# Banded attention by pairs of heads with block-diagonal keys

## What is computed

```python
def sliding_window_attention(q, k, v, sinks, rel_bias_table):   # S=512, BLOCK=WINDOW=128
    qb = q.reshape(B_, nb, BLOCK, Hkv, G, d)
    kb, vb = banded(k), banded(v)                # each block with the block before it: 256 keys
    logits = einsum('bnqkgd,bnskd->bnkgqs', qb, kb) * d ** -0.5
    logits = where(valid, logits + bias, -inf)   # bias by distance and head; valid: rel in [0, 128)
    m = maximum(max(logits, axis=-1), sink)
    p = exp(logits - m)
    p = p / (sum(p, axis=-1) + exp(sink - m))
    return einsum('bnkgqs,bnskd->bnqkgd', p, vb)
```

## Time and profile before

| what | value |
|---|---|
| median of 3 runs | 2322.81 us (2321.84 to 2324.82) |
| the profiled execution | 2321.14 us |
| its span | 2319.2 us |
| mean granted TensorE clock | 0.928 |
| PE busy | 2104.6 us (91%), 9984 instructions |
| DVE, ACT, POOL busy | 1028.7, 757.4, 157.8 us |

### The profile page before, as it was taken

The page is one execution under the profiler, slowest core; times in us unless marked ns, Lnnn a source line. Parts: engine busy times, 40 slices in busy tenths (PEclk is TensorE's granted clock), DMA queues, the critical chain, the costliest instruction groups (busy, mean ns, idle before and its releaser), DMA issues.

```text
span 2319.2 us, 25487 instructions
## 1 busy us (share of the span) xinstructions
PE 2104.6 (91%) x9984; PEld 1717.6 (74%) x9984; DVE 1028.7 (44%) x1463; ACT 757.4 (33%) x1130; POOL 157.8 (7%) x179
## 2 busy tenths in 40 slices
PE   6999999999999899999999998997439888999898
PEld 5865777888788687778887877775339666888786
DVE  4321434343336645344333345455543337665434
ACT  3125323222224455332222242434213224333322
POOL 2000000000002201000000022000002012000000
PEclk8989679999999999899999998999569999999998
DMA  5210012322232101132232223021020022223231
GB/s 167 91 37 0 1 55 84 97 90 90 91 105 71 58 19 37 37 93 91 90 106 86 98 73 101 19 63 47 18 55 1 1 73 73 90 90 105 76 101 44
DMA packets 137004, 158.11 MB, mean 68 GB/s; under 512 B 15832, under 2 KB 125408, under 8 KB 136928
## 3 DMA queue, kind: packets, MB, share of 16 engines
q1 hardware_dynamic: 135632, 155.01, 21.0%
q0 software_dynamic: 1296, 2.05, 0.3%
HBM read 153.36 MB, written 3.68 MB: 68 GB/s over the span
## 4 chain that ended last, share of the span: by engine, by line
PE 86%; DVE 8%; ACT 2%; POOL 1%; issue 1%; DMA 1%; SPq 0%; DVEq 0%; ACTq 0%; POOLq 0%
PE bank L2196 30%; PE bank L1940 16%; PE bank L2217 15%; PE bank L2016 4%; PE bank L2044 3%; PE bank L1964 3%; PE bank L2032 2%; PE bank L2081 2%; POOL arena L752 1%; PE bank L2175 1%; PE bank L2069 1%; PE bank L2092 1%; DVE XL L1278 1%; PE bank L2385 1%; PE bank L2414 1%
## 5 line engine op out<-in xcount | busy, mean ns | idle before, releaser
L2196 PE MATMUL bank<-XH,w_hi 128*128 128x512 f32 x1008 | 398.7, 396 | 0.0
L2196 PE MATMUL bank<-XH,w_lo 128*128 128x512 f32 x1008 | 393.4, 390 | 0.0
L2196 PE MATMUL bank<-XL,w_hi 128*128 128x512 f32 x1008 | 393.2, 390 | 0.0
L1940 PE MATMUL bank<-XH,w_hi 128*128 128x512 f32 x536 | 218.4, 408 | 16.1 <-DVE XL L1891 6.3
L2196 PEld LDWEIGHTS bank<-XH,w_hi 128*128 128x128 f32 x1008 | 189.2, 188 | 41.1 <-issue 0.5
L2217 PE MATMUL bank<-XH,w_hi 128*128 128x512 f32 x528 | 207.3, 393 | 12.9 <-DVE XL L1469 12.9
L2196 PEld LDWEIGHTS bank<-XH,w_lo 128*128 128x128 f32 x1008 | 189.2, 188 | 39.9
L2196 PEld LDWEIGHTS bank<-XL,w_hi 128*128 128x128 f32 x1008 | 189.4, 188 | 38.8 <-issue 0.5
L1940 PE MATMUL bank<-XL,w_hi 128*128 128x512 f32 x536 | 213.3, 398 | 0.0
L1940 PE MATMUL bank<-XH,w_lo 128*128 128x512 f32 x536 | 213.2, 398 | 0.0
L2217 PE MATMUL bank<-XL,w_hi 128*128 128x512 f32 x528 | 207.1, 392 | 0.0
(11 more groups left out here) (339 smaller groups left out, 3279.5 us busy)
## 6 DMA issues: line engine op xcount, KB each, us to landing
w_raw<-in_ffn_w_gate SPq DMA_DIRECT2D x22, 1024.0 KB, 5.3
w_raw<-in_ffn_w_up SPq DMA_DIRECT2D x22, 1024.0 KB, 5.3
w_raw<-in_ffn_w_down SPq DMA_DIRECT2D x22, 1024.0 KB, 4.9
w_raw<-in_w_up SPq DMA_DIRECT2D x22, 1024.0 KB, 5.1
w_raw<-in_w_in SPq DMA_DIRECT2D x13, 1024.0 KB, 5.3
w_raw<-in_w_down SPq DMA_DIRECT2D x11, 1024.0 KB, 4.9
w_raw<-in_even_w_in SPq DMA_DIRECT2D x9, 1024.0 KB, 5.4
w_raw<-in_even_w_out SPq DMA_DIRECT2D x4, 1024.0 KB, 5.2
```

The lines of the kernel that those rows point to most:

```text
L1940: m = pe.matmul(bank[L % 4][0:M, :], cols(w, k), x[:, x0 + k, :], start=(first_k and k == 0 and j == 0), stop=(last_k and k == kt - 1 and ...
L2196: m = pe.matmul(bank[b][:, :], w[:, k, P * c:P * (c + 1)], x[:, k, :], start=(k == 0 and j == 0), stop=(k == KT - 1 and j == 2))
```

## The change

For the banded attention a path of its own, `banded_attention`, on PE, DVE and ACT, with seven semaphores (wn_s, wn_m, wn_p, wn_t, wn_pt, wn_o, wn_on) in place of those of the shared `attention`.

- `kTb` becomes 2 x 512 columns: key head 0 in rows 0 to 63 of the first half, key head 1 in rows 64 to 127 of the second, the other rows zero (two fills at the start, and two writes instead of one).
- A step n is a pair of heads (pair, pair + 4) and one query tile i, so 16 steps. Its scores are one product of 128 rows: the tile of `qTb` with both heads against both halves of `kTb`, 512 columns, or 256 for the first query tile. The result is that of two products of 64 rows.
- DVE makes one scale-and-bias, one maximum and one small operation a step; the negated sinks are prepared at the start. ACT makes two exponentials a step, and the sink's two at the pair's last tile. Turns and value products are as many as before.
- At the end of a pair DVE adds, takes the reciprocal and scales in two operations, one for each key head.

The shared function loses its cases for "win"; these hunks are left out.

```diff
--- before.py
+++ after.py
...
@@ -400,7 +407,7 @@
         kTa = region(4 * SEQ, 4, SEQ)
         va = region(ST * 512, ST, 512)
         qTb = region(4 * SEQ, 4, SEQ)
-        kTb = region(SEQ)
+        kTb = region(2 * SEQ, 2, SEQ)
         vb = region(ST * P, ST, P)
         otok_e = region(ST * 512, ST, 512)
         winbias = region(8 * 256, 8, 256)
@@ -485,6 +492,10 @@
         rsum = small[:, 24:32].rearrange("p (a b) -> p a b", b=4)
         rinv = small[:, 32:36]
         esink = small[:, 36:44].rearrange("p (a b) -> p a b", b=4)
+        wmax, wneg, wsum, wsink = (small[:, at:at + 16].rearrange("p (a k i) -> p a k i", k=2, i=4)
+                                   for at in (74, 90, 106, 122))
+        nsinks = small[:, 138:146]
+        wrinv = small[:, 188:196].rearrange("p (k i) -> p k i", i=4)
         lam = small[:, 44:48]
         ssd = small[:, 138:154]
         mu1 = small[:, 56:70]
...
@@ -624,6 +631,14 @@
 
         def tok_units(stage):
             return [u for u in range(NU) if units[u][0] == stage]
+
+        def banded_keys(n):
+            pair, i = divmod(n, 4)
+            tiles = min(i + 1, 2)
+            return pair, i, tiles, slice(P * (i + 1 - tiles), P * (i + 1))
+
+        def by_key_head(x, tiles):
+            return x[:, 0:2 * P * tiles].rearrange("p (k s) -> p k s", k=2)
 
         def chunk(n):
             return slice(n * CH, (n + 1) * CH)
...
@@ -920,6 +933,35 @@
                     if n >= 1:
                         evacuate(n - 1)
                 evacuate(len(groups) - 1)
+
+            def banded_attention():
+                def evacuate(n):
+                    tiles = banded_keys(n)[2]
+                    act.wait_ge(wn_t, n + 1)
+                    if n >= 2:
+                        act.wait_ge(wn_o, n - 1)
+                    act.activation(PTb[:, n % 2, 0:2 * P * tiles], bank[3 + n % 2][:, 0:2 * P * tiles],
+                                   ACT.Copy).then_inc(wn_pt, 1)
+
+                for n in range(16):
+                    pair, i, tiles, _ = banded_keys(n)
+                    act.wait_ge(wn_m, n + 1)
+                    if n >= 3:
+                        act.wait_ge(wn_t, n - 2)
+                    if i == 0 and pair >= 2:
+                        act.wait_ge(wn_on, pair - 1)
+                    for k in range(2):
+                        if i == 3:
+                            act.activation(wsink[:, pair % 2, k, :], wneg[:, pair % 2, k, :], ACT.Exp,
+                                           bias=sinks[:, pair + 4 * k:pair + 4 * k + 1])
+                        last = act.activation(by_key_head(Pb[:, n % 3, :], tiles)[:, k, :],
+                                              by_key_head(Sb[:, n % 2, :], tiles)[:, k, :], ACT.Exp,
+                                              bias=wneg[:, pair % 2, k, i:i + 1],
+                                              accum_out=wsum[:, pair % 2, k, i:i + 1])
+                    last.then_inc(wn_p, 1)
+                    if n >= 1:
+                        evacuate(n - 1)
+                evacuate(15)
 
             def stick_breaking():
                 def ln_part(h):
@@ -979,7 +1021,7 @@
                 for u in qkv[1:] + tok_units("even_qb") + tok_units("even_kvb"):
                     split(u + 1)
                 stick_breaking()
-                attention("win")
+                banded_attention()
                 head_pairs_out("even", None)
                 residual("even_out", "ffn0")
 
...
@@ -1363,6 +1390,38 @@
                     if gi == 1 and h >= 1:
                         head_end(h - 1)
                 head_end(7)
+
+            def banded_attention():
+                def maxima(n):
+                    pair, i, tiles, _ = banded_keys(n)
+                    dve.wait_ge(wn_s, n + 1)
+                    if n >= 2:
+                        dve.wait_ge(wn_p, n - 1)
+                    to = by_key_head(Sb[:, n % 2, :], tiles)
+                    bias = winbias.rearrange("p (k h) s -> p k h s", k=2)[:, :, pair, 256 - P * tiles:256]
+                    link(dve.scalar_tensor_tensor(to, by_key_head(bank[n % 3], tiles), 0.125, bias, ALU.mult, ALU.add))
+                    link(dve.tensor_reduce(wmax[:, pair % 2, :, i:i + 1], to, AX.X, ALU.max))
+                    nsink = nsinks.rearrange("p (k h) -> p k h", k=2)[:, :, pair:pair + 1]
+                    dve.scalar_tensor_tensor(wneg[:, pair % 2, :, i:i + 1], wmax[:, pair % 2, :, i:i + 1], -1.0, nsink,
+                                             ALU.mult, ALU.min).then_inc(wn_m, 1)
+
+                def pair_end(pair):
+                    dve.wait_ge(wn_o, 4 * pair + 4)
+                    total = wsum[:, pair % 2, :, :]
+                    link(dve.tensor_tensor(total, total, wsink[:, pair % 2, :, :], ALU.add))
+                    link(dve.reciprocal(wrinv, total))
+                    o = bank[5 + pair % 2][:, :].rearrange("p (k i v) -> p k i v", k=2, v=64)
+                    dst = otok_e.rearrange("p i (k h v) -> p k i h v", k=2, v=64)
+                    for k in range(2):
+                        m = dve.tensor_tensor(dst[:, k, :, pair, :], o[:, k, :, :],
+                                              wrinv[:, k, :].unsqueeze(2).broadcast_to([P, 4, 64]), ALU.mult)
+                    m.then_inc(wn_on, 1)
+
+                for n in range(16):
+                    maxima(n)
+                    if n % 4 == 1 and n >= 4:
+                        pair_end(n // 4 - 1)
+                pair_end(3)
 
             def stick_breaking():
                 def softplus(h):
@@ -1406,6 +1465,9 @@
                 dve.tensor_scalar(subg, V("diff_subln_2", 0), 1.0 - LAM_INIT, None, ALU.mult)
                 dve.tensor_scalar(mu1, vec[:, vcol["mu_shift_2"]:vcol["mu_shift_2"] + 14], -1.0, 1.0, ALU.mult, ALU.add)
                 dve.tensor_scalar(ka1, vec[:, vcol["k_a_2"]:vcol["k_a_2"] + 4], -1.0, 1.0, ALU.mult, ALU.add)
+                dve.tensor_scalar(nsinks, sinks, -1.0, None, ALU.mult)
+                dve.memset(kTb[64:128, 0, :], 0.0)
+                dve.memset(kTb[0:64, 1, :], 0.0)
                 dve.wait_ge(bias_turned, 1)
                 dve.tensor_copy(brow[0:8, 0:384], bank[3][0:8, 0:384]).then_inc(bias_row_ready, 1)
                 L = lin_base["even"]
@@ -1437,7 +1499,8 @@
                     L += 1
                 split(qb[1] + 2)
                 dve.wait_ge(lin_ready, L + 1)
-                dve.tensor_tensor(kTb, bank[L % 4][:, :], rstd, ALU.mult).then_inc(lin_free, 1)
+                dve.tensor_tensor(kTb[0:64, 0, :], bank[L % 4][0:64, :], rstd[0:64, :], ALU.mult)
+                dve.tensor_tensor(kTb[64:128, 1, :], bank[L % 4][64:128, :], rstd[64:128, :], ALU.mult).then_inc(lin_free, 1)
                 L += 1
                 for t in range(4):
                     dve.wait_ge(lin_ready, L + 1)
@@ -2057,6 +2120,46 @@
                 values(N - 1)
                 pe.wait_ge(at_on, h0 + 8)
 
+            def banded_attention():
+                def scores(n):
+                    pair, i, tiles, keys = banded_keys(n)
+                    if n >= 3:
+                        pe.wait_ge(wn_m, n - 2)
+                    pe.matmul(by_key_head(bank[n % 3], tiles), qTb[:, pair, P * i:P * (i + 1)], kTb[:, :, keys],
+                              start=True, stop=True).then_inc(wn_s, 1)
+
+                def turn(n):
+                    tiles = banded_keys(n)[2]
+                    pe.wait_ge(wn_p, n + 1)
+                    if n >= 2:
+                        pe.wait_ge(wn_pt, n - 1)
+                    for j in range(2 * tiles):
+                        m = pe.transpose(bank[3 + n % 2][:, P * j:P * (j + 1)], Pb[:, n % 3, P * j:P * (j + 1)], ident)
+                    m.then_inc(wn_t, 1)
+
+                def values(n):
+                    pair, i, tiles, _ = banded_keys(n)
+                    pe.wait_ge(wn_pt, n + 1)
+                    if i == 0 and pair >= 2:
+                        pe.wait_ge(wn_on, pair - 1)
+                    for k in range(2):
+                        for j in range(tiles):
+                            c = P * (k * tiles + j)
+                            m = pe.matmul(bank[5 + pair % 2][:, 64 * (4 * k + i):64 * (4 * k + i) + 64],
+                                          PTb[:, n % 2, c:c + P], vb[:, i + 1 - tiles + j, 64 * k:64 * k + 64],
+                                          start=(j == 0), stop=(j == tiles - 1))
+                    m.then_inc(wn_o, 1)
+
+                scores(0)
+                scores(1)
+                for n in range(16):
+                    if n + 2 < 16:
+                        scores(n + 2)
+                    turn(n)
+                    if n >= 1:
+                        values(n - 1)
+                values(15)
+
             def stick_breaking():
                 def z(h):
                     b = base_of(h)
@@ -2157,8 +2260,8 @@
                 pe.wait_ge(winbias_ready, 4)
                 stick_breaking()
```

(29 more changed lines are left out.)

## The result

| | before | after |
|---|---|---|
| median | 2322.4 us (4 runs, 2321.84 to 2324.82) | 2305.31 us (4 runs, 2303.54 to 2308.90) |
| ratio | | 0.9926, 95% interval 0.9909 to 0.9944 |
| profiled execution, span | 2321.14, 2319.2 us | 2305.24, 2303.4 us |
| mean granted clock | 0.928 | 0.936 |

A forecast was written before the change was run, and what follows sets the result against it. PE at half clock was taken to bound the banded attention. Savings of 30.5 (stage) + 1.7 (output's turn) + 1.3 (even_out) = 33.5 us from 2321.1 gave 2287.6, as a median 2289 us; range 2283 to 2302.

The forecast's parts named there:

- The bound, PE at half clock: Banded attention: PE busy 59.50 of 59.52 us at granted clock 0.50, so PE bounds the stage.
- The rows decide the clock: Banded stage: clock follows how much of the array products fill; with 128-row scores full clock holds from the start.
- The terms of PE's work: Banded stage at full clock: scores 12.8 us, turns 6.2, values 11.8, together 30.8 us.
- Does another engine take over: Banded stage, full step: PE 2.19 us, DVE 2.00, ACT 1.94 at most, so PE stays the bound, by little.
- a pair's end (1.3) fits into the rest: Banded stage: scores issue 4.38 us before their turns; DVE 1.67 and ACT 1.10 leave 1.6 spare for 1.3 us.
- Rival 3: Banded steps don't overlap because of buffer and copy waits: 5.6 us a step, time 2347 us; chance 0.04.
- Head and tail: Banded stage: pipeline filling and end cost 2.2 us of waits, the last pair's end 1.3 us.
- The output's turn and even_out: Behind the banded stage: full clock saves 1.7 us in the turn and 1.3 in even_out, with bounds 0 and 2.6.
- What stands before the stage: Ahead of the banded attention: start still at 240.18 us, new fills covered by DVE's 10.30 us wait for PE.
- The median's 1.7 above the profiled execution: Whole kernel: median of runs taken as 1.7 us above the profiled execution, making 2287.6 into 2289 us.
- Rival 2: Banded stage: full clock, but DVE or ACT sets the step, or clock comes late; 2293 to 2300 us, chance 0.12.

The follow-up runs named there:

- experiment 1: Kernel after with only rows 0 to 63 of queries and keys in each step's score product, second head's scores left out; 2323.81 us, ratio 1.0004.
- experiment 7: Kernel before, 64-row products, with five unread products in each of PE's two waits at the start of the banded attention; 2300.83 us, ratio 0.9910.
- Experiments 3: Kernel after with the pair's end on DVE placed one step later, nothing else; 2298.45 us, ratio 0.9899.
- experiment 4: Kernel after with six unread 512-column products before the turns of step 4p + 6, in PE's idle time at pairs' ends; 2300.11 us, ratio 0.9903.
- experiment 6: Kernel after with later pair end, later sink exponentials, and unread products filling the output turn's waits; 2292.35 us, second row of runs 2293.90 us.
- experiment 8: Kernel of experiment 6 with zero-padded 128-row keys in stick-breaking too; 2278.82 us, in a second layout 2276.61 us (ratio 0.9804).
- experiment 2: Kernel before with the block-diagonal zero-padded keys alone, old loop head by head, 128-row score products; 2301.90 us, ratio 0.9913.

## Why the prediction was wrong

- **The bound, PE at half clock:** right. In the stage DVE and ACT work as long at either clock, and experiment 1, with half clock back, gives back the whole gain.
- **The rows decide the clock:** right in what it said of this change, shown by one change of rows in one product (experiment 1). Too strong as I worded it, "whether the products fill the array": experiment 7 shows that at 64 rows too the clock holds, once it is not lost at the start. And one rival stands untested. Score products of 64 rows are not only emptier, they also make the 128-row products beside them longer (the mask 0.26 us and not 0.06), and those of 66 rows don't, though they fill hardly more of the array. The diff attention with its 66 rows comes back after 3.3 us. So it may be the change between 64-row and 128-row products, and not the rows filled, that keeps the clock down; a banded stage with 66 rows would tell, and no run has it. What is shown is that 128-row products in place of 64-row ones bring the clock back. The Trainium skill, "TensorE: Matmul & The Clock Gate", section "What's actually happening", which lets only being busy count, has nothing for this difference: with 64 rows PE is busy 63.5 of 65.0 us at a granted clock of 0.52, with 128 rows 39.0 of 46.7 us at 0.85. The measurement decides. On idle gaps, of which the same page of the Trainium skill warns in the section "HAM oscillation — how this bites in real kernels", the traces agree in kind: the three gaps of the kernel after are each followed by half clock, and filled they are not. The waits in the Trainium skill's example there, for transfers, are longer than these (1.7, 1.7 and 2.2 us).
- **The terms of PE's work:** right to the hundredth. 0.91, 0.44 and 0.84 us in the chain at 251 to 253 us. A product of two padded halves costs what one contiguous product does.
- **Does another engine take over, and "a pair's end (1.3) fits into the rest":** this step failed. DVE's own work was sized well: 0.69 and 0.69 for the wide operations (688 ns), 26.0 us in the stage where about 30 were forecast. But I counted the pair's end as 1.3 us of work and left out that it first waits for PE's values of the pair's last step (DVE idle 1.6 us), with the maxima of the next step queued behind it. Rival 3 named DVE's wait for buffers and not this one. The time to spare was too large as well: 4.38 us from a step's scores to its turns holds between full steps, but at a pair's end the short step with 256 columns stands between, and there PE is ready after 3.3 us (253.80 to 257.1), which leaves 0.5 us and not 1.6 for an end of 1.3. Experiments 3 and 4 size it: 3.8 us of gaps, and 5.9 us of clock that falls behind them. Of the last I had no term at all: I asked only whether the clock would hold at the start.
- **Head and tail, 3.5 us:** low. With the pair's end and the sink out of the way the stage is 35.85 us, 5.0 above PE's 30.8; PE still waits 1.8 us for ACT.
- **The output's turn and even_out, 3.0:** taken as likely; 0.4 came. The clock can be kept full there (experiment 6), but the time from there to the end was hardly shorter for it.
- **What stands before the stage:** forecast as unchanged. It moved by 2.9 us with the places where the clock fell at the start and in stick-breaking; my range allowed for such things only at its low end. That was bad luck; without it the time would be about 2302.4, an estimate, at the edge of the range, with the forecast of the stage as wrong as it is.
- **The median's 1.7 above the profiled execution** was 0.1 for this kernel.
- Rival 2 (full clock, but DVE or ACT sets the step, or the clock comes late), at 2293 to 2300, was the nearest in its number, but neither of its causes came: DVE and ACT are within a full step's time, and the clock is full from the start. It falls later, behind the pairs' ends.

## What to carry to other kernels

When PE is busy and its granted clock is half, look first at the clock row and not at the instructions: here a layout that fills 128 rows with zeros, or ten products at the right place that nobody reads, was worth about 20 us. When one engine gets twice as fast, go through every wait of the others again, in queue order: an instruction that waits for the sped-up engine holds back what stands behind it, and that gap can cost more in clock than in idle time. Put such an end behind the work that is already ready.

## What the runs showed of the hardware that was not expected

- Products of 64 rows between products of 128 cost extra on both sides: the mask product behind 64-row scores is 0.26 us on the chain and 0.06 behind 128-row ones, and the 384-column product between two masks 0.84 against 0.70 (fences of experiment 8). At half clock the 512-column score product is 2.00 with 64 rows (experiment 1) and 1.81 with 128 (kernel after). Products of 66 and 96 rows show none of it: the mask 0.06, the 384 columns 0.65 and 0.70.
- Rows of keys that hold only zeros are enough to change the granted clock: 0.52 with 64 rows (experiment 1), 0.94 with 128 of which 64 are zero (experiment 2). No run has all 128 rows of the keys filled.
- Where the clock falls can differ between executions of the same instructions: with the same instructions ahead of it, the banded stage began at 240.1 us (experiment 4) and at 243.1 (kernel after), with 30.7 and 34.1 us of half clock ahead of it.
